# Recurrent jobs of a two-layer trunk: one operand product of the next job to a slot, a second copy of the local output and the second pair of key turnings in later slots

## The reference, cut to what matters

```
def wkv_scan(r, w, kk, a, k, v, S0, reverse):
    ...
    xs = (tm(r), tm(w), tm(-kk), tm(kk * a), tm(k), tm(v))

    def step(S, inp):
        r_t, w_t, a_t, b_t, k_t, v_t = inp
        sa = jnp.einsum('bhvk,bhk->bhv', S, a_t)
        S = S * w_t[:, :, None, :] + sa[..., None] * b_t[:, :, None, :] + v_t[..., None] * k_t[:, :, None, :]
        return S, jnp.einsum('bhvk,bhk->bhv', S, r_t)
```

## Time and profile before

| | us |
|---|---|
| median of 3 runs | 1950.82 (1950.69 to 1952.63) |
| the profiled execution, its time | 1949.46 |
| its span in the trace | 1947.7 |
| PE busy | 1880.9 (97%) |
| DVE busy | 1097.0 (56%) |
| ACT busy | 725.3 (37%) |
| POOL busy | 146.0 (7%) |

### The profile page before, as it was taken

The page is one execution under the profiler, slowest core; times in us unless marked ns, Lnnn a source line. Parts: engine busy times, 40 slices in busy tenths (PEclk is TensorE's granted clock), DMA queues, the critical chain, the costliest instruction groups (busy, mean ns, idle before and its releaser), DMA issues.

```text
span 1947.7 us, 41559 instructions
## 1 busy us (share of the span) xinstructions
PE 1880.9 (97%) x18459; PEld 1694.0 (87%) x18459; DVE 1097.0 (56%) x2002; ACT 725.3 (37%) x1326; POOL 146.0 (7%) x140
## 2 busy tenths in 40 slices
PE   6998999999999999999999989999999999999998
PEld 3984445999999999999998678888689999999998
DVE  4826654565555562254465766767677555557223
ACT  2325554343332341142345644444324332334211
POOL 1000000000000000000002533333000000000000
PEclk9999999999999999999999999999999999999999
DMA  9227657122122222322221000000212122212322
GB/s 336 69 87 249 239 181 251 44 87 87 46 85 87 73 60 60 90 83 88 66 65 43 7 4 4 4 4 4 93 44 87 44 87 87 87 44 62 88 62 82
DMA packets 143443, 164.21 MB, mean 84 GB/s; under 512 B 2512, under 2 KB 108288, under 8 KB 143264
## 3 DMA queue, kind: packets, MB, share of 16 engines
q1 hardware_dynamic: 140992, 154.03, 24.5%
q0 software_dynamic: 2272, 7.52, 1.1%
HBM read 157.79 MB, written 3.75 MB: 83 GB/s over the span
## 4 chain that ended last, share of the span: by engine, by line
PE 86%; DVE 6%; DMA 2%; ACT 2%; POOL 2%; issue 2%; SPq 0%; POOLq 0%; DVEq 0%; ACTq 0%
PE ps L227 81%; DMA ring<-in_ada_w 1%; DMA work<-in_ada_w 1%; POOL work L2925 1%; PE ps L1404 1%; DVE ring L2803 1%; PE ps L2557 1%; DVE work L517 1%; DVE small L1540 1%; POOL work L2927 1%; PE ps L2159 1%; DVE x_lo_r L523 0%; ACT work L1468 0%; PE ps L2535 0%; DVE work L2821 0%
## 5 line engine op out<-in xcount | busy, mean ns | idle before, releaser
L227 PE MATMUL ps<-x_hi_r,w_lo 128*128 128x320 f32 (+3 forms) x2272 | 526.9, 307 | 0.4 <-issue 0.4
L227 PE MATMUL ps<-x_hi_r,w_hi 128*128 128x320 f32 (+2 forms) x1792 | 428.7, 311 | 0.9 <-issue 0.9
L227 PE MATMUL ps<-x_lo_r,w_hi 128*128 128x320 f32 (+2 forms) x1792 | 424.8, 308 | 0.0
L227 PEld LDWEIGHTS ps<-x_hi_r,w_lo 128*128 128x128 f32 (+1 forms) x2272 | 378.2, 187 | 1.8 <-issue 0.5
L227 PEld LDWEIGHTS ps<-x_lo_r,w_hi 128*128 128x128 f32 x1792 | 305.6, 188 | 0.0
L227 PEld LDWEIGHTS ps<-x_hi_r,w_hi 128*128 128x128 f32 x1792 | 303.7, 188 | 1.4 <-issue 1.3
L227 PE MATMUL ps<-work 64*64 64x64 f32 (+10 forms) x3284 | 265.6, 273 | 15.6 <-ACT work L1468 6.7
L227 PEld LDWEIGHTS ps<-work 64*64 64x64 f32 (+5 forms) x3284 | 168.9, 148 | 90.7 <-issue 60.4
L760 DVE SCALAR_TENSOR_TENSOR work<-ps,par,work 128x511 f32<-128x511 f32 (+1 forms) x188 | 103.4, 550 | 255.6 <-ACT work L927 245.7
L927 ACT ACTIVATE work<-ps,par 128x640 f32<-128x640 f32 x88 | 77.8, 884 | 377.9 <-PE ps L227 377.9
L804 ACT ACTIVATE w_hi<-ring 128x1024 fp32r<-128x1024 f32 (+1 forms) x152 | 135.6, 937 | 204.5 <-DMA ring<-in_ffn_down 184.5
(11 more groups left out here) (413 smaller groups left out, 2616.7 us busy)
## 6 DMA issues: line engine op xcount, KB each, us to landing
ring<-in_ada_w SPq DMA_DIRECT2D x22, 2048.0 KB, 8.0
ring<-in_ffn_up SPq DMA_DIRECT2D x44, 1024.0 KB, 7.1
ring<-in_ffn_down SPq DMA_DIRECT2D x16, 1408.0 KB, 6.9
ring<-in_l_w_in SPq DMA_DIRECT2D x11, 1024.0 KB, 5.2
ring<-in_l_w_out SPq DMA_DIRECT2D x4, 2048.0 KB, 8.3
ring<-in_l_w_in SPq DMA_DIRECT2D x3, 2048.0 KB, 7.8
work<-in_ada_w SPq DMA_DIRECT2D x2, 2048.0 KB, 15.9
h<-in_xT SPq DMA_DIRECT2D x1, 2560.0 KB, 10.2
```

The lines of the kernel that those rows point to most:

```text
L227: return pe.matmul(out, lhsT, rhs, start=first, stop=last)
```

## The change

Two tables change. In `BESIDE`, prod 1 and yi 1 go from slot 6 to slot 7, prod 2 from slot 7 to slot 8, and prod 3 and 4 from slot 8 to slot 9, behind chain 2. In `ONCE` the turnings of the third head pair go from slot 7 to slot 9. No instruction is added or taken away.

```diff
@@ BESIDE: entries 6 to 10
-            (("chain", -1, 0), ("prod", 1, 0), ("yi", -1, 0), ("prod", 1, 1), ("yi", -1, 1), ("chain", -1, 1)),
-            (("prod", 1, 2), ("vt", 1, 0)),
-            (("prod", 1, 3), ("prod", 1, 4)), (("chain", -1, 2), ("vt", 1, 1)), (("atok", 1, 0),),
+            (("chain", -1, 0), ("prod", 1, 0), ("yi", -1, 0), ("chain", -1, 1)),
+            (("prod", 1, 1), ("yi", -1, 1), ("vt", 1, 0)), (("prod", 1, 2),),
+            (("chain", -1, 2), ("prod", 1, 3), ("prod", 1, 4), ("vt", 1, 1)), (("atok", 1, 0),),
@@ ONCE
-        ONCE = {2: (("turn", 1, 0), ("turn", 1, 1)), 7: (("turn", 2, 0), ("turn", 2, 1)), 10: (("spread", 3, 0),),
+        ONCE = {2: (("turn", 1, 0), ("turn", 1, 1)), 9: (("turn", 2, 0), ("turn", 2, 1)), 10: (("spread", 3, 0),),
```

## The result

The changed kernel takes 1958.96 us (median of 6 runs, 1955.29 to 1961.55), the kernel before 1950.76 us (median of 6 runs, 1950.08 to 1952.63): the ratio is 1.0037, 95% interval 1.0027 to 1.0047. It is slower, by about twice what was forecast, and outside the range. Of the 12.1 us, 11.4 lie in jobs 1 to 6 and 0.9 in job 0 (37.48 us from 1108.08 to 1145.56, where before had 36.57), so most of the difference is where the forecast put it.

The account below looks back on a forecast made before the run. DVE's list up to prod 4, in a closed loop per job, was taken as the bound. Six jobs at 0.59 (3.54) plus 0.40 in job 0, less 0.2, gave 3.7 on 1950.82: 1954.5 us, range 1950.5 to 1956.5.

Parts of the forecast that it names:

- the chain through prod 4, the BK copy, atok and gram 0: Closed loop per job over DVE, ACT, PE and POOL to x0, claimed to have no waits to spare.
- the mask of v(3,1) and chain 2: Two DVE pieces newly ahead of prod 4, 0.40 and 0.19 us, delaying jobs 1 to 6 by 0.59 us each.
- the 0.2 us taken off job 0 for its clock: Part of job 0's added 0.40 us comes back, as work pushed behind the 1.2 GHz stretch runs at 2.4 GHz.
- Rival A: Gram 0 hangs on PE's own order, so the saved waits of 0.94 and 0.56 us count; about 1945 us, chance 0.10.
- Rival B: Job 0's low PE clock vanishes or falls into idle time, winning back 1.7 us; result +2.0, 1952.8 us, chance 0.20.
- rival C: The delay is absorbed by slack between prod 4 and x0; nothing measurable, 1950.8 us, chance 0.10.
- the earlier addition: DVE adds xt(2,1) sooner, so PE's 0.94 us wait ahead of v(3,1) moves to atok; costed at nothing.
- jobs 1 to 6 alike: Sign expected in the profile after: each step from x0 to x0 is 0.4 to 0.7 us longer, equally in these jobs.
- Rival D: DVE's mask of v(3,0) waits for PE in even-next jobs, prod 2 lengthens in odd ones; +5.5, 1956.3 us, chance 0.12.
- the 0.1 us that was worked out from the shared ports: Prod 2 on DVE, issued nearer POOL's first copy, lengthens by 0.1 us in each of three jobs, 0.3 us in all.
- Slower by over 0.2%: Outcome of more than about 3.9 us slower; chance 0.36, from 0.24 of the main case and 0.12 of more waits.
- The main case: Late prod 4 makes the whole kernel 3.7 us slower, 1954.5 us; chance 0.48.

Follow-up runs that it names:

- (3): Kernel before with only prod 3 and prod 4 put behind the mask of v(3,1) and chain 2; 1956.73 us, ratio 1.0034.
- (5): Changed kernel plus 3 (even next job) or 7 (odd) idle identity products on PE ahead of the wait for prod 4; 1956.01 us, ratio 1.0021.
- (10): Changed kernel unaltered, timed again beside the kernel before on that chip; 1960.02 us, ratio 1.0040.
- (6): Kernel before with yi 1 moved to slot 8, behind prod 4; 1946.90 us, ratio 0.9981.
- (4): Kernel before with slots 6 and 7 as changed, prod 2, 3 and 4 in slot 8 ahead of the mask of v(3,1), turnings in slot 7; 1957.61 us.

## Why the prediction was wrong

**What held.** That the chain through prod 4, the BK copy, atok and gram 0 sets the job's step; that prod 4 would come later by the mask of v(3,1) and chain 2; and that it reaches x0 in full. The forecast had 0.59 us a job and 3.7 us in all. At a full clock (3), (5) and (10) show +0.60, +0.59 and +0.58 us in job 1, an even-next one, and (3) and (5) +0.40 and +0.48 in job 2, an odd-next one, where in the changed order prod 3 comes past POOL's copies. Over jobs 1 to 6 it is +3.9 us in the trace of (3) and +2.8 in that of (5), and +3.9 by the mean of the runs of (5) at equal mean clock. (6) shows the same rule the other way round: pieces taken from ahead of prod 4 are won in full.

The term that no run shows is the 0.2 us taken off job 0 for its clock. Job 0 was forecast 0.2 us longer and took 0.9 us more at the same mean clock (0.91), and 36.45 us at 0.95 in (10), 0.1 less than before: its clock moves it more than the terms of the sum do.

**Rival A** fell: in the changed kernel PE reached atok early and stood there 1.83 us until prod 4 had ended. In (4), in job 1, prod 4 was as early as before and PE's 0.60 us ahead of v(3,1) were gone, and the step stayed at 33.38 us. **Rival B** did not happen in the trace, where job 0 had its low clock as before, and **rival C** fell with (3) and (6).

**The step that failed** is the one that costed the earlier addition at nothing: "The wait is not gone, it moves to the front of atok". The move itself was foreseen, 2.3 us ahead of atok (it measured 1.83, with 0.36 left ahead of xt(3,0)). What it does to PE's clock was not: the step puts that at nothing without a reason. I looked at the clock in rival B alone, in job 0 alone, and with one sign alone, as something that could be won back. The runs show the other sign: the granted clock went to half (2.4 to 1.2 GHz) in each of jobs 1 to 4 of the profiled run, and the mean clock was 0.9923 over the six runs of the changed kernel, where that of the kernel before was 0.9944 over 27 runs; in (10) it was 0.9907 against 0.9937. As an estimate, 0.0021 x 1958 = 4.1 us of PE's time were lost, and 5.9 us in (10), at most, since not all of it is on the path. By the means of the runs the changed kernel lies 7.5 us above before (7.9 in (10)) and the one with the filler 3.9. So 3.9 us come from the late prod 4 and 3.6 to 4.0 from the clock; by the medians it is 4.9 and 3.3, and the intervals of the two ratios overlap, so the split is good to a microsecond or two. That the clock costs time is shown twice, by the filler and by the two traces of the same kernel. How it splits between more waiting and waiting in one place is less sure. (3) has the more and not the gathering (0.9928), (4) the gathering and in its even-next jobs not the more (0.9913); both lie below before, the gathering lower. In (4), though, prod 4 was late in the odd-next jobs, so it does not hold the gathering alone.

The forecast sign "jobs 1 to 6 alike" did not come for the same reason: in the trace the steps grew by 0.6 us (job 6) to 2.9 us (jobs 2 and 4), in step with the clock.

The Trainium skill (TensorE: Matmul & The Clock Gate, part 1) says that an idle PE is the state of the low clock and that activity lifts it. The trace agrees in job 2: behind waits of 0.36, 1.83 and 0.51 us, with work between them, the clock was granted at 0.50. But the waits do not settle it: in job 1 the same three waits stood ahead of a fall in one trace and ahead of none in the other (10). That sentence stood in the prediction beside job 0 alone; half-speed stretches came in job 0 and jobs 1 to 4 of the one trace, and in job 0 and jobs 2 to 6 of the other.

**Rival D** happened in part. In job 2 the mask of v(3,0) found PE ready (no idle time before L2816 at 1198.39 in the DVE rows). In job 5 it did not. DVE in the trace of after, in order of time, there:

```profile
1305.37 0.49 DVE L2860 COPY merged<-ps 128x320 f32<-128x320 f32 x1
1306.01 0.49 DVE L2816 TENSOR_TENSOR work<-ps,work 128x320 f32<-128x320 f32 x1
```

With starts 0.64 us apart and a copy of about 0.4 in its place elsewhere, DVE waited some 0.24 us there. In job 1 it waited nowhere there. That is a small part of the result, but it is of the kind that the rival named. Prod 2 beside POOL's copy took 1.24 us instead of 1.14, which is the 0.1 us that was worked out from the shared ports, and prod 3 won 0.12 back. (4) and (6) show the whole size of that contention: the pair of prod 2 and prod 3 took 2.57 us with both copies beside it and 1.63 with none. The Trainium skill (SBUF — State Buffer, section Who interferes with whom) has the later of the two blocked until the first is done; the trace agrees: prod 2 ended 0.68 us behind the end of the first copy (1200.03 and 1199.35), nearly a full undisturbed 0.73, and the second copy, 1.19 us beside prod 2, takes 0.71 alone; it ended 0.57 us behind prod 2 (1200.60), so it was held back, though not by the whole 0.71. POOL in job 2 after the change:

```profile
1198.63 0.72 POOL L2934 COPY work<-work 64x640 f32<-64x640 f32 x1 [2.89 <-DVE merged L2861]
1199.41 1.19 POOL L2935 COPY work<-work 64x640 f32<-64x640 f32 x1
```

**The chances.** Slower by over 0.2% had 0.36. The main case itself lay just under that bound, and a case "the clock falls in more jobs" was missing on the slow side.

## What to carry to other kernels

Where one engine's list sets the pace, what counts is which pieces stand ahead of the one that releases the others: take pieces from there, and check for each what another engine's list needs of it (chain 1 cost 15 us against its 0.10). A wait of PE that is "only moved" is not free where the granted clock has already been seen to fall in one repetition of the loop: before costing it at nothing, look at the granted clock in each repetition, in more than one trace if there are, and compare kernels with the mean clock of their runs beside the times. Useless matmuls sized to the wait are a good test for it, and their duration must be read from the trace first.

## What the runs showed of the hardware

A 128x128 fp32 product by the identity, issued as a matmul, took 0.24 us with its neighbours (3.62 us for 15), where I had reckoned 0.11 from the starts of the transposes: the 15 products are 30 passes in the trace. The same unchanged kernel ran between 1945.11 and 1956.39 us, at mean clocks between 0.998 and 0.992: where the half-speed stretches fall differs from run to run as well, as the two traces of the changed kernel show (jobs 1 to 4, and jobs 2 to 6), and a single trace of a kernel shows one such case. In job 1 of that kernel the fall of the clock made the first 18 passes of gram 0 take 2.38 us instead of 1.36.
